# One encoder layer on eight cores: stages joined on one memory map, with projections issued between attention steps

## The reference

```python
h = rms_norm(x, g_mix)
qa, ka, va, qb, kb, vb, qm, gate_logits = split(h @ w_in)     # 8960 columns
oa = banded_attention(rms(qa), rms(ka), va, alibi, 128, sink=sink_a)
ob = dilated_attention(rms(qb), rms(kb), vb, alibi)           # groups weighted by their denominators
om = memory_attention(rms(qm), rms(mk), mv)                   # mk, mv from rms_norm(mem) @ w_mem_kv
y_br = einsum('nsbc,bcd->nsbd', stack(oa, ob, om), w_branch)
x = x + sum(sigmoid(gate_logits + b_gate) * y_br) @ w_out
x = x + square(relu(rms_norm(x, g_mlp) @ w_up)) @ w_down
```

## Time and profile before

| | us |
|---|---|
| median of 3 runs (lowest, highest) | 3298.91 (3297.16, 3299.38) |
| span of the profiled execution, slowest core (core 5) | 3298.9 |
| the same, other cores | 3269.7 to 3294.8 |
| PE busy, of the span | 2684.3 (81%) |
| DVE, ACT, POOL busy | 1415.1, 1221.6, 388.1 |

### The profile page before, as it was taken

One profiled execution on the slowest core, in us unless ns is written; L12 is line 12 of the kernel. 1 busy time (PEld: TensorE's weight loads), 2 busy tenths in 40 slices (PEclk: granted clock), 3 DMA queues, 4 the chain that ended last, 5 costly groups with the idle time before them and its releaser, 6 DMA issues.

```text
span 3298.9 us, 46240 instructions; the slowest of 8 cores (3269.7 to 3298.9 us)
## 1 busy us (share of the span) xinstructions
PE 2684.3 (81%) x14284; PEld 1285.1 (39%) x14284; DVE 1415.1 (43%) x2305; ACT 1221.6 (37%) x2206; POOL 388.1 (12%) x338
## 2 busy tenths in 40 slices
PE   3599999999999991665563628999479999999998
PEld 2353334433344440332352513444234444444443
DVE  5478973589800001553272725665212123212321
ACT  6245530255643331887765631222212112111210
POOL 0000000000000000000164645444000000000000
PEclk9999999999999995998896858999789999999999
DMA  6523223322232217112675846664861101110110
GB/s 230 72 79 90 65 90 92 87 77 71 77 107 87 89 74 162 38 40 92 186 209 152 229 140 224 236 230 172 173 120 64 64 1 64 64 50 15 64 52 26
DMA packets 259292, 350.91 MB, mean 106 GB/s; under 512 B 29296, under 2 KB 217456, under 8 KB 251248
## 3 DMA queue, kind: packets, MB, share of 16 engines
q1 hardware_dynamic: 224176, 305.23, 27.8%
q0 software_dynamic: 34880, 42.73, 8.5%
HBM read 261.68 MB, written 128.97 MB: 118 GB/s over the span
## 4 chain that ended last, share of the span: by engine, by line
PE 68%; ACT 8%; DMA 7%; issue 7%; DVE 5%; POOL 2%; SPq 1%; another core or an unknown queue 1%; ACTq 0%; DVEq 0%; POOLq 0%
PE p_acc L404 19%; PE p_upp L1074 13%; PE p_acc_0 L1087 7%; PE p_acc_1 L1087 7%; PE p_acc L415 6%; PE p_ybr L937 5%; PE p_N L571 2%; ACT t_E L550 2%; PE p_acc_0 L959 2%; PE p_ssp L454 2%; DVE t_cpb L425 2%; PE p_acc_1 L959 2%; PE p_Dn L571 2%; DMA t_ksl<-sKB 2%; DMA t_wt<-w_in 1%
## 5 line engine op out<-in xcount | busy, mean ns | idle before, releaser
L404 PE MATMUL p_acc<-t_hT,t_wt 128*128 128x512 bf16 x3648 | 829.9, 379 | 2.5 <-DMA t_wt<-w_in 2.1
L404 PEld LDWEIGHTS p_acc<-t_hT,t_wt 128*128 128x128 bf16 x3648 | 355.1, 97 | 404.0 <-issue 3.4
L1074 PE MATMUL p_upp<-t_h2Tt,t_wup 128*128 128x512 bf16 x2048 | 446.1, 381 | 37.7 <-DMA t_wup<-w_up 37.7
L1078 ACT ACTIVATE t_rl<-p_upp 128x512 f32<-128x512 f32 x256 | 152.8, 597 | 757.0 <-PE p_upp L1074 750.2
L456 ACT ACTIVATE t_lnb<-p_ssp 128x512 f32<-128x512 f32 x268 | 160.1, 597 | 456.1 <-PE p_ssp L454 439.2
L1074 PEld LDWEIGHTS p_upp<-t_h2Tt,t_wup 128*128 128x128 bf16 x2048 | 201.0, 98 | 281.5 <-issue 41.8
L1079 DVE TENSOR_TENSOR t_upT<-t_rl 128x512 bf16<-128x512 f32 x256 | 177.3, 693 | 310.4 <-ACT t_rl L1078 310.4
L475 DVE SCALAR_TENSOR_TENSOR t_stg<-p_acc,t_par,t_lnb 128x512 bf16<-128x512 f32 x264 | 242.4, 918 | 38.0 <-ACT t_lnb L458 28.8
L1087 PE MATMUL p_acc_0<-t_wdn,t_upT 128*128 128x512 bf16 x1024 | 228.8, 382 | 36.3 <-DMA t_wdn<-w_down 24.1
L550 ACT ACTIVATE t_E<-p_S 128x512 bf16<-128x512 f32 (+3 forms) x548 | 217.7, 452 | 99.4 <-PE p_S L536 85.0
L571 PE MATMUL p_Dn<-t_PT,t_ones 128*128 128x128 bf16 (+3 forms) x1160 | 237.9, 258 | 0.0
(11 more groups left out here) (104 smaller groups left out, 2688.0 us busy)
## 6 DMA issues: line engine op xcount, KB each, us to landing
sGT<-t_stg SPq DMA_DIRECT2D x24, 1024.0 KB, 3.9
t_gTt<-sGT SPq DMA_DIRECT2D x8, 3072.0 KB, 22.4
t_wt<-w_in POOLq DMA_DIRECT2D x17, 1024.0 KB, 11.9
t_xt<-x SPq DMA_DIRECT2D x8, 2048.0 KB, 10.2
t_x<-y SPq DMA_DIRECT2D x8, 2048.0 KB, 8.1
y<-t_x SPq DMA_DIRECT2D x8, 2048.0 KB, 6.6
sKB<-t_stg SPq DMA_DIRECT2D x12, 1024.0 KB, 3.9
sVB<-t_vst SPq DMA_DIRECT2D x24, 512.0 KB, 2.9
```

Source lines behind the costliest of these rows:

```text
L404: i = h.matmul(a[:, :], lhsT=w[:, kc, u["wcol"]:u["wcol"] + 128], rhs=rhs[:, kc, t * TT:(t + 1) * TT], start=(kc == 0), stop=(kc == 7))
L1074: ins = h.matmul(U[:, :], lhsT=wup[:, kc, c * 128:(c + 1) * 128], rhs=hT_[:, kc, :], start=(kc == 0), stop=(kc == 7))
```

## The change

`barrier()` is gone. All tiles lie at addresses written by hand in one arena, and `Ctx.place` gives a new tile the waits of whatever lay there before. DRAM tensors have buffers too, so that a load waits for the store it needs. PSUM is eight named banks, and a reader of a bank now also waits for the other engines that read it. What is moved:

- The norm of token tile t+1 is issued between the units of tile t, for the rows KA, VA, QA and KB of group 0; then come the memory's, and the other 24 rows. The squares of every second feature unit are taken on ACT. V of branch A stays on chip (`VA2`, 128 columns instead of 256, with ones beside it).
- The 96 V units are issued by `Pump.step()` between the steps of A and M, the 192 gate units between those of B: after the scores of step i, before the PV of step i-2. A gate is now a Tanh on ACT and a multiply-add on DVE, and its 512 tokens are stored at once by an SP transfer of their own.
- Attention has two banks for S, `LAG` 2, four P and two E buffers. In A the two side blocks of a group are one item, so a group has three items, not four (192 in all), and V with ones beside it gives numerator and denominator of a head in one matmul of half the columns. B's ring has three buffers (`RB = 3`), and its transfers are issued from another step.
- `wbr` and `wout` lie where `hT` lay, so they are loaded when the last gate unit is done, not during A. The final division of half 2 (`b_final(1)`) comes after the first two merge steps. `wup` lies over `wbr`, `wout` and a gate tile and waits for these alone.

```diff
-    def barrier(self):
-        for e in self.engs:
-            for f in self.engs:
-                if f is not e and f.count > 0:
-                    self._wait(e, (f.sem, f.count, f))
-            for s in self.slots:
-                if s.count > 0:
-                    self._wait(e, (s.sem, s.count, None))
...
+        before = [b for lo, hi, bs in self.placed if lo < off + n and off < hi for b in bs]
+        bufs = []
+        for i in range(nbuf):
+            b = Buf("%s_%d" % (name, i))
+            for o in before:
+                for tok in ([o.w] if o.w is not None else []) + list(o.r.values()):
+                    had = b.r.get(tok[0].key)
+                    if had is None or had[1] < tok[1]:
+                        b.r[tok[0].key] = tok
+            bufs.append(b)
...
+        for t in range(NTT):
+            n0 = len(units)
...
+            js = list(range(4 * t + 4, 4 * t + 8))
+            for i, j in enumerate(js):
+                us[i]["after"].append(lambda j=j: n_square(j))
+                us[5 + i]["after"].append(lambda j=j: n_scale(j))
+                us[7 + i]["after"].append(lambda j=j: n_trans(j))
+            us[4]["after"].append(lambda js=js: n_rstd(js[0], js[-1] + 1))
+            if t + 1 < NTT:
+                us[8]["after"].append(lambda js=js: [n_load(j + 4) for j in js])
...
+                if ui % 2 == 0:
+                    cx.op(act, lambda h: h.activation(out=q[:], in_=a[:, :], func=AF.Square), reads=[ba], writes=[bq])
+                else:
+                    c_, bc = cpb[0], b_cpb[0]
+                    cx.op(dve, lambda h: h.tensor_copy(out=c_[:], in_=a[:, :]), reads=[ba], writes=[bc])
+                    cx.op(dve, lambda h: h.tensor_tensor(out=q[:], in0=c_[:], in1=c_[:], op=ALU.mult),
+                          reads=[bc], writes=[bq])
...
-        NS = 4
+        NP, NE = 4, 2
+        PT, b_PT = zip(*[place("PT%d" % i, [128, 512], BF16, 185 + i) for i in range(NP)])
...
+            def mm(h):
+                for kc in range(8):
+                    ins = h.matmul(a[:, :], lhsT=w[:, kc, 128 * c:128 * c + 128], rhs=hT[:, kc, t * TT:(t + 1) * TT],
+                                   start=(kc == 0), stop=(kc == 7))
...
+            th, bth = tgb[i], b_tgb[i]
+            go, bgo = gob[i], b_gob[i]
+            cx.op(act, lambda h: h.activation(out=th[:], in_=a[:, :], func=AF.Tanh, scale=0.5,
+                                              bias=par[:, P_HALFB + j:P_HALFB + j + 1]),
+                  reads=[ba, b_par], writes=[bth])
+            cx.op(dve, lambda h: h.tensor_scalar(out=go[:], in0=th[:], scalar1=0.5, scalar2=0.5,
+                                                 op0=ALU.mult, op1=ALU.add), reads=[bth], writes=[bgo])
+            cx.dma(sp, bgo, GT[j][:, t * TT:(t + 1) * TT], go[:], reads=[bgo], writes=[b_GT[j][t]])
+
...
+            def step(self):
+                self.due += self.rate
+                while self.i < len(self.us) and self.i + 0.5 <= self.due:
+                    self.us[self.i]()
+                    self.i += 1
...
-            LAG = NS - 1
+        def run_attention(items, hook, pump, sbanks, LAG=2):
+            n = len(items)
+            for i in range(n + LAG):
+                for f in hook.get(i, []):
+                    f()
...
+                pump.step()
+                if i >= LAG:
+                    it = items[i - LAG]
+                    P_, bP = it["P"], it["bP"]
+                    flush(force_bank=it["bank"], grp=it["grp_id"])
+
+                    def pv(h):
...
-                        pv=([(nv[:, :, qs - q0:qe - q0], VAd[:, kc, kvh * 128:kvh * 128 + 128]),
-                             (dv[:, :, qs - q0:qe - q0], ones128[:])] if nq == QTA else
-                            [(nv[:, 0, qs - q0:qe - q0], VAd[:, kc, kvh * 128:kvh * 128 + 128], 0, nq),
-                             (dv[:, 0, qs - q0:qe - q0], ones128[:], 0, nq),
-                             (nv[:, 1, qs - q0:qe - q0], VAd[:, kc, kvh * 128:kvh * 128 + 128], nq, nq),
-                             (dv[:, 1, qs - q0:qe - q0], ones128[:], nq, nq)]),
+                V0 = lambda kc: VA2[:, kc, kvh, 64:192]
+                V1 = lambda kc: VA2[:, kc, kvh, 0:128]
...
+                for kc, b0 in ((k0, 128), (k0 + 1, 0)):
+                    its.append(dict(common, nq=512, s_list=[(KK(kc), q_[:, c, :, :], 0, 2)],
+                                    mask=[(blocks(512, 2), WAt[:, 2 * c:2 * c + 2, b0:b0 + 256])], mask_bufs=[b_wat],
+                                    pv=[(nb[:, 0:256], V0(kc), 0, 256), (nb[:, 256:512], V1(kc), 256, 256)],
+                                    starts=[kc == k0, False], stop=False))
...
+                for idx, (e, sl) in enumerate(sides):
+                    kc = k0 - 1 if e == 0 else k0 + 2
+                    qo = 0 if e == 0 else 128
+                    s_list.append((KK(kc), q_[:, c, :, qo:qo + 128], 256 * idx, 2))
+                    pv.append((nb[:, qo:qo + 128], V0(kc), 256 * idx, 128))
+                    pv.append((nb[:, 256 + qo:256 + qo + 128], V1(kc), 256 * idx + 128, 128))
+                s0 = sides[0][1]
+                its.append(dict(common, nq=256 * len(sides), s_list=s_list,
+                                mask=[((lambda n: lambda T: T[:, 0:256 * n].rearrange("p (s b q) -> p s b q", s=n, b=2))
+                                       (len(sides)), WEt[:, s0:s0 + len(sides), 2 * c:2 * c + 2, :])],
...
+        vpump = Pump(v_units, n_a + n_m - 4)
+        run_attention(items, hook, vpump, [2, 3])
...
-        RB = 4
+        RB = 3
...
+        def b_final(S2):
+            for q4 in range(4):
+                lo, hi = q4 * 512, (q4 + 1) * 512
+                cx.op(act, lambda h: h.activation(out=Dacc[:, :, lo:hi], in_=Dacc[:, :, lo:hi], func=AF.Ln),
+                      reads=b_dacc, writes=b_dacc)
+                cx.op(act, lambda h: h.activation(out=Dacc[:, :, lo:hi], in_=Dacc[:, :, lo:hi], func=AF.Exp, scale=-1.0),
+                      reads=b_dacc, writes=b_dacc)
+                for hh in range(4):
+                    e = dve if hh % 2 == 0 else pool
+                    cx.op(e, lambda h: h.tensor_tensor(out=oB[:, hh, :], in0=Nacc[:, hh, lo:hi], in1=Dacc[:, hh, lo:hi],
...
+                t0 = S2 * 2048 + lo
...
+        gpump = Pump(g_units, len(halves[0][0]) + len(halves[1][0]) - 8)
+        for S2, (items, hook) in enumerate(halves):
+            starts = sorted(hook)
+            hook2 = {}
+            for si, st in enumerate(starts):
+                at = (starts[si - RB + 1] + 3) if si >= RB else 0
+                assert at <= st
+                hook2.setdefault(at, []).extend(hook[st])
+            run_attention(items, hook2, gpump, [2, 3])
...
+        wbr, b_wbr = place("wbr", [128, 12, D], BF16, 2, 3)
+        wout, b_wout = place("wout", [128, 8, D], BF16, 26, 2)
+        for i in range(3):
+            cx.dma(pool, b_wbr[i], wbr[:, 4 * i:4 * i + 4, :],
+                   w_br_d[512 * i:512 * (i + 1), :].rearrange("(kc p) n -> p kc n", p=128), writes=[b_wbr[i]])
+        for i in range(2):
...
+        p3_og_loads(0)
+        p3_x_loads(0)
+        for dc in range(2):
+            merge_step(0, dc)
+        b_final(1)
+        gTt[1], b_gTt[1] = place("gT1", [128, 24, TT], BF16, 82)
...
+        p3_og_loads(1)
+        for dc in range(2, 8):
+            merge_step(0, dc)
...
+        wup, b_wup = place("wup", [128, 8, 4096], BF16, 2, 4)
+        wdn, b_wdn = place("wdn", [128, 32, D], BF16, 66, 4)
+        for i in range(4):
+            cx.dma(pool, b_wup[i], wup[:, :, 1024 * i:1024 * (i + 1)],
+                   w_up_d[:, 1024 * i:1024 * (i + 1)].rearrange("(kc p) n -> p kc n", p=128), writes=[b_wup[i]])
```

1216 lines of the change are left out of this document (579 added, 637 removed).

## The result

The changed kernel takes 3153.24 us (median of 4 runs, 3149.73 to 3164.88) against 3299.14 us for the kernel before in the same comparison: a ratio of 0.9565, 95% interval 0.9548 to 0.9582. It is faster, by 146 us. The prediction was 369 us, its range 2820 to 3065; so the direction was right and 223 us of the gain are missing. None of the prediction's accounts gives this time: even the loose one, 3076, is 77 us short of it. In some executions of these kernels some of the cores are granted 0.81 of the clock in dense stages where the others have 1.00, and take some per cent longer; all times, ratios and stages here are from executions or cores without that.

The account below looks back on a forecast made before the run. The prediction took PE's instruction list, with its nearly empty stretches and waits inside attention, to bound the kernel. Its stage terms, 609 + 39 + 243 + 10 + 88 + 16 + 530 + 38 + 392 + 965, gave 2930 us, range 2820 to 3065.

Parts of the forecast that it names:

- the loose one: Rival for the total: two-bank coupling costs in A and B, and full tile waits in group 2; 3076 us, chance 0.19.
- that fear: Rival in B: Exp and Tanh need different ACT tables, two loads per gate, 493 us; total 3198, chance 0.01.
- the 4.5 named: Sign in A: the prediction is wrong if a group takes over 4.5 us; its own figure was 3.8.
- the named signs: Signs: PE 95% busy or more from about 30 to 609 us; wrong if B's clock falls below 0.9.
- 350 lie in groups 0 and 1; I add 5% there: B: of 447 us of PE work, 350 lie in groups 0 and 1, with 19 us added for POOL's part.
- the 61 us of tile waits in group 2: B, group 2: PE waits 3.6 us for a tile behind a late gate, at six in ten of 28 tiles.
- the ledger: Whole kernel: the new program's time as PE sees it, stage by stage, summed to 2930 us.
- PE sets 1.97 per unit with a small wait: Feature units: PE sets the rate at 1.97 us each, 378 us for 192 units.
- The mean of 0.92 for the product: Feature units: the product's 0.92 us in the 2.0 us that a unit asks of DVE.
- the merged matmul 41 us: A: numerator and denominator sharing a matmul takes 192 x 512 columns, 41 us, off PE.
- the whole term of 243: A with 74 V units: 3.8 us per group, 64 groups, 243 us in place of 219.
- the 38 us between the halves: Between B's halves: the division alone, each quarter waiting for the last one's store, and a tile's load; 38 us, was 43.

Follow-up runs that it names:

- e9: Changed kernel with four gate tiles in place of two and each gate store issued two gate units later; 3028 us.
- e1: Changed kernel with each feature unit's product issued one unit later on DVE, behind the next cast and square; 3135 us, ratio 0.952.
- e6: Changed kernel with six accumulator banks for feature units, B's loads one step earlier and no gates in group 2; 3099 us, ratio 0.9431.
- e5: Changed kernel with late product, six accumulator banks, third score bank in A, four gate tiles, B's loads one step earlier, early `t_h2Tt`; 3012 us, single execution.
- e13: Changed kernel with e5's edits except early `t_h2Tt`, plus separate division buffers, second half's tiles loaded earlier, gate stores two units later, second `oB`; 2924 us.
- e8: Changed kernel with all V units ahead of A, all gates behind B, A's denominators made a second time, two numerator banks; 3342 us, ratio 1.0135.
- e3: Changed kernel with the gate stores issued by ACT in place of SP; 3141 us, ratio 0.9526.
- e15: Changed kernel with all V units done ahead of A; 3285 us, ratio 0.996.

## Why the prediction missed

*The stages and their order: right.* The waits and releasers that were named are in the trace: the scores of group 2 behind `t_ksl`, the idle stretch at `b_final(1)`, `t_wup` issued right on the last projection (2184.59). ACT loads tables five times in all, so nothing came of that fear, and A's group took 4.05 us, under the 4.5 named. But two of the named signs show where the miss is: PE is 83% busy in the norm part and 92% in the feature units, not 95% or more, and the clock of B fell below 0.9 in its first half.

*The step that failed first: "350 lie in groups 0 and 1; I add 5% there", and the 61 us of tile waits in group 2.* The mechanism was named (a load behind a gate's store) but sized as single waits of 3.6 us at six in ten of 28 tiles. Three things were measured in its place. There are 20 waits with 94.5 us in sum, because load, score, gate and store close a ring. There are 26.6 us of waits on `t_PT`, because the store's landing holds DVE, which was not foreseen. And there are about 40 us more of busy time, most of them the clock: the prediction assumed full clock at full load and did not ask what the waits would do to it, though it named the sign. In sum, the ledger had 447 us of PE's work and 80 of waiting for B's halves. Measured are 460 us of work (as in e9), 40 of slower work and 123 of waiting. With the ring opened B's halves take 482 us (e9).

*The second step that failed: "PE sets 1.97 per unit with a small wait". It is 2.20.* It was counted from nine matmuls of 0.2157 and the 25 us of idle time that the window showed. The earlier trace rows already had the answer: 771 us for the stage, less 166 for B's V and an estimated 28 for A's (256 matmuls of 256 columns, half of 0.2157 each), is 577 for 268 units, 2.15 each. PE's busy share overstates what it does, since a matmul that follows a wait is shown with its full latency of 0.38 us, not 0.2157. The mean of 0.92 for the product mixed two forms (0.75, and 1.10 where the output is strided). And the engines' loads were compared one by one, where a line through three of them was the limit: that is what e1, e6 and e5 show. The norm part missed in part for the same reason; of its 32 us some 9 are won by late product and banks (e5), the rest stays open.

*Branch A: within 17 us, by luck.* The prediction let PE nearly bound it and gave the merged matmul 41 us. It is worth 14 at most, and A without any V unit takes 248, more than the whole term of 243.

*Between the halves, after B, and the end: right in kind, 47 us short in sum.* The terms given for the 38 us between the halves add up to 36. The division's quarter was 6.2 us in them and is 8.6, as Ln and Exp do not run beside the products. After B the first merge was 12 us later than the 29 said and the next wait 8 longer than the 20. The 29.9 us from `t_wup` to PE's start were taken from the earlier trace rows, where 37.7 us of loading stood before a PE that then had `t_h2Tt` in place; now `t_h2Tt`, 1 MB issued 7.4 us behind the weights, landed 45 us later. Cured alone it gives nothing (e5).

That e13 lands at 2924, next to the forecast, is luck and does not make the ledger right: B with its gap is 73 us under its terms there, the part up to the last feature unit 23 over, the stretch from there to B 8, and from B's end on 34 over.

## What to carry to other kernels

When a store is put on a queue with loads, ask what the store waits for. The issuer goes in order, so it passes one engine's delay on to everything behind it; four buffers with a store issued later were worth 125 of the 229 us that all edits together won. Look for closed lines through several engines, not for the fullest engine. When one is opened, the next limit (banks, a single output tile) may hide the gain until it goes too. And take a stage's rate from its length over its count, not from instruction costs and busy shares.

## What the runs showed of the hardware

The granted clock follows PE's long waits, in both directions. B without gates had 0.61 over its length, gap included, and needed 230 us of PE time for its attention (e8). With 192 gates among the same matmuls and few long waits it had 0.93 with the gap and 0.97 in the halves (e9). The Trainium skill, TensorE: Matmul & The Clock Gate, "HAM oscillation — how this bites in real kernels", describes it: a wait for a transfer lets the array fall to the low clock, and the next burst starts cold. The traces agree: gate matmuls after such a wait took 0.43 us each, 0.2157 otherwise. Between the changed kernel and e9 it makes a wait cost about 1.4 times its length (139 us won in B, 101 of them idle). Short waits did not do it: e3 has 108 us of them at 0.98. Filling idle PE time with work that has to be done anyway gives back clock beside the time. Where PE does not set the rate, the clock seems to be worth little: A without V units took 248 us at 0.57 (e15), and 250 at 0.99 with 192 matmuls more (e8).
